# Modulation columns of the first attention in three ranges, and a new order of steps on the engines around both attentions

## What is computed

```python
c_act = jax.nn.silu(c)
for i in range(DEPTH):                       # DEPTH = 2
    mod = (c_act @ w_ada[i] + b_ada[i])[:, None, :]
    sh_a, sc_a, g_a, sh_m, sc_m, g_m = jnp.split(mod, N_MOD, axis=-1)
    h = x * (1.0 + sc_a) + sh_a
    y = diff_attention(h, ...) if i % 2 == 0 else sliding_window_attention(h, ...)
    x = layer_norm(ALPHA * x + (1.0 + g_a) * y, ln_mix_g[i], ln_mix_b[i])
    h = x * (1.0 + sc_m) + sh_m
    y = squared_relu_mlp(h, w_up[i], w_down[i])
    x = layer_norm(ALPHA * x + (1.0 + g_m) * y, ln_mlp_g[i], ln_mlp_b[i])
return x
```

## Time and profile before

| | us |
|---|---|
| median of 3 runs (2266.6 to 2270.5) | 2270.3 |
| the profiled execution | 2269.6 |
| its span, first to last instruction | 2267.5 |
| PE busy in the span | 2196.9 (97%) |
| DVE busy | 1636.5 (72%) |
| ACT busy | 987.8 (44%) |
| mean granted TensorE clock | 0.992 of full |

### The profile page before, as it was taken

The page is one execution under the profiler, slowest core; times in us unless marked ns, Lnnn a source line. Parts: engine busy times, 40 slices in busy tenths (PEclk is TensorE's granted clock), DMA queues, the critical chain, the costliest instruction groups (busy, mean ns, idle before and its releaser), DMA issues.

```text
span 2267.5 us, 26074 instructions
## 1 busy us (share of the span) xinstructions
PE 2196.9 (97%) x10140; PEld 1822.1 (80%) x10140; DVE 1636.5 (72%) x1734; ACT 987.8 (44%) x1334; POOL 33.9 (1%) x53
## 2 busy tenths in 40 slices
PE   5899999999999999999999899999999999999997
PEld 5777888887888888888887688877888888888885
DVE  5888888887887686778686888886664455564557
ACT  0134444445433443443444646536533443443542
POOL 0000000000000000000000000000000000000000
PEclk9989999999999999999999999999999999999999
DMA  9978888877998989799876765566666676666673
GB/s 373 385 284 324 319 314 295 305 238 268 332 334 287 334 318 323 268 348 328 311 256 197 243 227 201 195 194 196 223 223 219 207 241 205 213 214 220 220 230 110
DMA packets 253583, 596.42 MB, mean 263 GB/s; under 512 B 13378, under 2 KB 14740, under 8 KB 253204
## 3 DMA queue, kind: packets, MB, share of 16 engines
q1 hardware_dynamic: 244688, 578.86, 73.4%
q10 hardware_dynamic: 8772, 15.89, 2.2%
HBM read 592.60 MB, written 2.10 MB: 262 GB/s over the span
## 4 chain that ended last, share of the span: by engine, by line
PE 89%; DVE 6%; DMA 2%; issue 1%; ACT 1%; ACTq 0%; POOL 0%; DVEq 0%; POOLq 0%
PE pair L1572 24%; PE pair L1574 24%; PE pair L1573 24%; DVE acc L859 1%; PE pair L1842 1%; PE pair L1844 1%; PE pair L1843 1%; PE turn L1477 1%; DVE w_lo L837 1%; PE pair L1592 1%; PE turn L1916 1%; PE turn L1897 1%; DMA sink<-in_b_sinks_dram 1%; PE pair L1594 1%; PE pair L1593 1%
## 5 line engine op out<-in xcount | busy, mean ns | idle before, releaser
L837 DVE TENSOR_TENSOR w_lo<-raw,w_hi 128x1024 fp32r<-128x1024 f32 x712 | 851.7, 1219 | 261.6 <-ACT w_hi L470 255.0
L470 ACT ACTIVATE w_hi<-raw 128x1024 fp32r<-128x1024 f32 x712 | 729.1, 1058 | 601.3 <-PE pair L1574 420.4
L1572 PE MATMUL pair<-w_hi,h_hi 128*128 128x512 f32 x1456 | 581.1, 399 | 3.3 <-DVE w_lo L837 3.3
L1574 PE MATMUL pair<-w_hi,h_lo 128*128 128x512 f32 x1456 | 568.7, 391 | 0.0
L1573 PE MATMUL pair<-w_lo,h_hi 128*128 128x512 f32 x1456 | 567.7, 390 | 0.0
L1572 PE MATMUL pair<-w_hi,f_hi 128*128 128x512 f32 x1056 | 413.9, 392 | 0.0
L1574 PE MATMUL pair<-w_hi,f_lo 128*128 128x512 f32 x1056 | 411.2, 389 | 0.0
L1573 PE MATMUL pair<-w_lo,f_hi 128*128 128x512 f32 x1056 | 410.8, 389 | 0.0
L859 DVE SCALAR_TENSOR_TENSOR acc<-ada_w,cvec,acc 128x1024 f32<-128x1024 f32 x300 | 383.5, 1278 | 0.1
L1572 PEld LDWEIGHTS pair<-w_hi,h_hi 128*128 128x128 f32 x1456 | 274.0, 188 | 60.0 <-DVE w_lo L837 4.2
L1574 PEld LDWEIGHTS pair<-w_hi,h_lo 128*128 128x128 f32 x1456 | 273.7, 188 | 58.4
(11 more groups left out here) (184 smaller groups left out, 1651.4 us busy)
## 6 DMA issues: line engine op xcount, KB each, us to landing
ada_w<-in_w_ada_dram SPq DMA_DIRECT2D x320, 512.0 KB, 6.0
raw<-in_w_up_dram SPq DMA_DIRECT2D x128, 1024.0 KB, 5.5
raw<-in_w_down_dram SPq DMA_DIRECT2D x128, 1024.0 KB, 5.3
raw<-in_a_w_qkv_dram SPq DMA_DIRECT2D x48, 1024.0 KB, 7.2
ada_f<-in_w_ada_dram SPq DMA_DIRECT2D x44, 512.0 KB, 11.3
raw<-in_b_w_qkv_dram SPq DMA_DIRECT2D x20, 1024.0 KB, 5.2
raw<-in_a_w_o_dram SPq DMA_DIRECT2D x16, 1024.0 KB, 6.1
raw<-in_b_w_o_dram SPq DMA_DIRECT2D x16, 1024.0 KB, 5.2
```

The costliest lines, as they stand in the source:

```text
L470: act.activation(w_hi[:, (b.n * SUB + n) % SPLITS], raw[:, slot, k:k + 2], ACT.Copy).then_inc(hi_ready, 1)
L837: dve.tensor_tensor(w_lo[:, slot, k:k + 2], raw[:, slot, k:k + 2], w_hi[:, (b.n * SUB + n) % SPLITS].bitcast(F32), ALU.subtract).then_inc( ...
L1572: pe.matmul(o, hi[:, kt, at], w[:, k], start=kt == 0, stop=False)
L1574: mm = pe.matmul(o, lo[:, kt, at], w[:, k], start=False, stop=kt == KT - 1)
```

## The change

**Start.** The modulation is made in six streams instead of four: shift and scale of columns 0 to 7 in pieces of one row tile by 1024 columns as before, then shift and scale of columns 8 to 11, and of 12 to 15, in pieces of two row tiles by 512 columns, still 512 KB each. There are six `sum_end`, the last four with 4 matmuls each. The pieces that PE takes are listed by number. DVE adds a piece of the later streams with two 512-wide instructions that are linked by a semaphore. Subtiles 8 to 11 need columns 8 to 11, and 12 to 15 need 12 to 15. h of chunks 2 and 3 is handed over in halves. ACT splits 6 subtiles, not 4, before the first `first_hi`. x is loaded in two halves. The loads of the layer-norm vectors and biases move from ACT's queue to SP's, behind the first 12 pieces, and those of mask and rope tables to SP's behind piece 47; the exponential of the condition runs on ACT before the lambda and sink loads are issued. PE takes pieces 1, 4, 7, 10 before it turns the vectors.

**Elsewhere.** DVE's `block_` runs its hooks ahead of the `ada_tile`. Around the second attention two affine steps move behind `rope_k`, `rope_q` runs behind the unit steps of its subtile, and PE's and ACT's steps for the turned q move by one subtile.

```diff
+PRE_STREAMS = [(0, 0, 8), (1, 0, 8), (0, 8, 4), (1, 8, 4), (0, 12, 4), (1, 12, 4)]
+PE_PIECES = [1, 4, 7, 10, 17, 20, 23, 26, 34, 37, 41, 44, 50, 53, 57, 60]
+def pre_subtile(s):
+    if s < 8:
+        return s // 4, s % 4
+    return (s - 8) // 2 % 2, 4 + 2 * ((s - 8) // 4) + s % 2
+FIRST_SPLITS = 6
+FIRST_ADA = [6, 7]
...
             # SP
-            load_pre(16)
-            sp.dma_start(x[:], ...)
-            load_pre(14)
-            load_half(0, 0)
-            load_pre(4)
-            load_half(0, 1)
-            load_pre(6)
-            load_half(0, 2)
-            load_pre(6)
-            load_half(0, 3)
-            load_pre(14)
-            load_half(1, 0)
-            load_pre(4)
...
+            load_pre(PRE_SLOTS)
+            sp.wait_ge(cleared, 2)
...
+            load_pre(12)
+            load_x(0)
+            load_pre(8)
+            load_half(0, 0)
+            load_half(0, 1)
+            load_x(1)
+            load_half(0, 2)
+            load_half(0, 3)
+            load_pre(9)
+            load_half(1, 0)
+            load_pre(3)
+            load_half(1, 1)
+            load_pre(4)
...
+            load_pre(11)
+            load_half(1, 2)
+            load_pre(5)
+            load_half(1, 3)
...
             # ACT
-            block_(n1=HALF)
+            block_(n1=FIRST_SPLITS)
             first_hi(0)
             first_hi(1)
-            block_(n0=HALF)
-            block_(n1=2)
+            block_(n0=FIRST_SPLITS)
+            block_(n1=4)
             first_hi(2)
-            block_(n0=2, n1=3)
+            block_(n0=4, n1=6)
             first_hi(3)
...
             # DVE, pre_tile
+                for k, kt in enumerate(kts):
+                    src = pre_view(n)[:, k]
+                    if kt == 0:
+                        ins = dve.tensor_scalar(dst, src, cvec[:, 0:1], None, ALU.mult)
+                    else:
+                        if k == 0:
+                            dve.wait_ge(ada_added, ADA_SLOTS + BY_PE + n - pe_pieces(n))
+                        ins = dve.scalar_tensor_tensor(dst, src, cvec[:, kt:kt + 1], dst, ALU.mult, ALU.add)
+                    if k < len(kts) - 1:
+                        link(ins)
+                ins.then_inc(ada_added, 1)
...
             # DVE, block_
+                    if hooks and n in hooks:
+                        hooks[n]()
                     for m in ada:
                         if m == n:
                             ada_tile()
-                    if hooks and n in hooks:
-                        hooks[n]()
...
             # DVE, the start
+            tiles(16)
...
+            lambda_dots()
+            tiles(5)
+            pre_out(0)
+            lambdas()
+            tiles(11)
+            pre_out(1)
+            first_scale(0, 8)
             first_u(0)
             first_u(1)
             first_lo(0)
             block_(n1=2)
             first_lo(1)
+            block_(n0=2, n1=FIRST_SPLITS)
+            tiles(6)
+            block_(n0=FIRST_SPLITS, n1=7)
+            tiles(3)
+            pre_out(2)
+            block_(n0=7)
             tiles(4)
+            constants()
+            block_(n1=4)
             tiles(3)
+            pre_out(3)
+            first_scale(8, 4)
+            first_u(2)
+            first_lo(2, 0, 2)
+            first_lo(2, 1, 2)
+            tiles(10)
+            pre_out(4)
             tiles(4)
+            block_(n0=4, n1=6)
+            tiles(2)
+            pre_out(5)
+            first_scale(12, 4)
             first_u(3)
+            first_lo(3, 0, 2)
+            first_lo(3, 1, 2)
+            block_(n0=6, ada=FIRST_ADA, hooks={7: lambda: rope_qk(0, 0, SUB + 6)})
...
             # PE, from the second sum_end on
             sum_end(1)
             sum_begin(2)
+            for s in range(3):
+                half_subtile(s)
+            sum_piece(34)
+            half_subtile(3)
             sum_piece(37)
             pe.wait_ge(x_taken, 2)
             half_subtile(4)
+            pe.wait_ge(x_loaded, 32)
+            first_turn(2)
+            half_subtile(5)
             sum_end(2)
             sum_begin(3)
+            sum_piece(41)
+            half_subtile(6)
+            sum_piece(44)
+            half_subtile(7)
+            sum_end(3)
+            sum_begin(4)
+            half_subtile(8)
+            half_subtile(9)
+            pe.wait_ge(x_taken, 4)
+            first_turn(3)
+            sum_piece(50)
             sum_piece(53)
+            sum_end(4)
+            sum_begin(5)
             sum_piece(57)
+            sum_piece(60)
+            half_subtile(10)
+            half_subtile(11)
+            sum_end(5)
+            for s in range(12, 16):
                 half_subtile(s)
...
             # second attention: ACT, DVE, PE
-            block_(hooks={0: load_affine(2), 1: load_affine(3), 4: load_qkv_bias(0), 5: v_place, 6: k_turned(0), 7: k_turned(1)})
+            block_(hooks={0: load_affine(2), 1: load_affine(3), 5: v_place, 6: k_turned(0), 7: k_turned(1)})
...
-            block_(before=rope_k, at=3, ada=ADA_B[1], hooks={2: affine(2, 2), 5: affine(2, 3)})
+            block_(before=rope_k, at=3, ada=ADA_B[1], hooks={4: affine(2, 2), 6: affine(2, 3)})
...
-                block_(before=first, at=3, ada=ADA_B[2 + i], hooks={4: second}, beside=attend_b)
+                block_(ada=ADA_B[2 + i], hooks={3: lambda: first(49 + i, (49 + i) % 2), 4: second}, beside=attend_b)
...
-                       hooks={1: turn_pair(R_b, 0, q_there(i)), 2: turn_pair(R_b, 1, q_there(i))})
+                       hooks={2: turn_pair(R_b, 0, q_there(i)), 3: turn_pair(R_b, 1, q_there(i))})
```

## The result

The changed kernel is slower than before and slower than forecast: 2275.2 us (median of 10 runs) against 2270.3, a ratio of 1.0024 with a 95% interval of 1.0016 to 1.0033, so 0.2%. The executions of the kernel before fall into two groups (of 83 on record 22 took 2266.4 to 2267.7 us and 56 took 2269.4 or more), so that single executions of one kernel can lie almost 4 us apart. The forecast was 2267.3; the time lies just past the upper end of the range, where rival B stood.

What follows compares the result with a forecast made beforehand. The kernel was taken as PE's work plus its waits and lower-clock time. Start +2.4, first attention -2.1, second -2.6 give -2.3 on 2267.5, a span of 2265.2, with 2.1 around it 2267.3 us; range 2256 to 2275.

Steps and rivals of the forecast that it cites:

- rival B: Start: PE stands still ahead of subtiles 8 and 12, more runs at the lower clock; block 2 at 159, 2275 us; chance 0.16.
- +5.0 for the clock: Subtile 8 to block 2: 5.0 us added for lower clock in one-column matmuls and a turn, bounds 0 and 8.
- Third weight tile at 61.7, PE at 67.2: Until the first subtile: tile arrives at 61.7, splits and h follow, PE starts at 67.2, 6.3 us earlier.
- the credit of 0.6 for the stretch at 249 GB/s: Loads before the first subtile: earlier DVE start recovers 0.6 of 2.0 us lost at slack queues, bounds 0 and 2.0.
- Until the sum of stream 3: Start: `sum_end(2)` at 90.4, DVE's list of 13.9 us behind it, PE standing still from 100.4 to 105.5.
- Subtile 8 at 109.5: Start: after stream 3's sum, 0.9, and 3.1 us for bias, scale, half chunks of h and `first_lo`, subtile 8 begins at 109.5.
- The stage's upper end of +8: Until block 2: stage sum +2.4 us, range -4 to +8, including 4 for low clock at the fourth group and sums.
- Pieces in two parts: DVE in the start: a piece of two linked 512-wide instructions takes 1.5 us, between 1.39 and 1.7.
- First attention -2.1, second -2.6: Attentions: moved hooks remove PE's waits of 1.2 and 0.9; affine work behind `rope_k` removes 2.5, net -2.6 there.
- Base of the sum: Whole kernel: terms were added to the profiled span of 2267.5 us; the runs' median, 0.7 above, was left in the range.
- A: Start: stream 3 is ready after subtile 7 and the clock holds; block 2 at 139 to 141, 2256 us; chance 0.22.
- C: Attentions: nothing gained beyond the 2.1, since work moved behind `rope_k` returns at the first q; 2269.9 us; chance 0.14.

Runs made afterwards that it cites:

- e_split4: The changed kernel with ACT splitting four subtiles, not six, ahead of the first `first_hi`: 2273.0 us, ratio 1.0004 to 1.0023 against the kernel before.
- e_dve: The changed kernel with three `w_lo` and the constants on DVE moved from ahead of the fourth modulation sum to behind h of chunk 2: 2272.5 us.
- e_sum2: The changed kernel with PE's third modulation sum one subtile and one turn earlier, right after subtile 4: 2272.7 us.
- e_inter: The changed kernel with PE's pieces 50, 53, 57 and 60 each between subtiles instead of in two pairs: 2269.1 us.
- e_hooks: The kernel before with only DVE's hooks moved ahead of the `ada_tile`, second attention unchanged: 2267.1 us.
- e_attn: The kernel before with only the edits outside the start: hooks ahead of the `ada_tile` and the moved steps of the second attention: 2264.6 us.
- c_all: The changed kernel with the edits of e_split4, e_sum2, e_dve and e_inter together: 2264.4 us, ratio 0.9965 to 0.9983 against the kernel before.

## Why the prediction was wrong

The steps that failed are the price of the lower clock until block 2, put at 5.0 us beside the low subtiles, to which the runs added 6.0 (1.0, 2.1 and 2.9 below), and the third weight tile, 2.1 us late.

- **Third weight tile at 61.7, PE at 67.2.** Failed, by 2.1 and 2.0. The chain behind the tile was right (5.5 us forecast, though its terms add up to 5.3, and 5.4 measured). What failed is the credit of 0.6 for the stretch at 249 GB/s, taken because DVE starts earlier. DVE did start 5.9 us earlier, but then stood 7.1 us for pieces, since the queues moved less. By the stretches, relative to 405 GB/s, before lost 2.3 us from 10 to 25 and after 3.8; with the credit that is the 2.1. I had bounded this at 0 from below. The start was nevertheless not where the time went: e_split4 gave PE 4.1 us and kept 1.8.
- **Until the sum of stream 3.** Right in mechanism and size. `sum_end(2)` began at 91.56 (90.4), DVE waited 5.08 (6), its list lasted 14.2 (13.9), PE stood still for 4.85 (5.1). e_dve and e_sum2 show that the order on DVE makes this wait.
- **Subtile 8 at 109.5.** 111.74: 1.3 are left of the late start at `sum_end(3)`, and 1.0 comes since the sum behind the wait ran at the lower clock (1.86 for 8 matmuls, where the one at 91.56 took 0.95), which I had left to the upper bound.
- **+5.0 for the clock.** The term that was mis-sized, in two places. Until `sum_end(5)` 27.7 were forecast and 29.8 measured: the 13.6 us at the lower level there, with PE busy throughout, cost 6.8 where I had 5.0, and subtile 8 took 0.3 more. And I gave subtile 8 its 4.7 behind a wait, but took the last four at 10.9, though subtile 12 stands behind the same wait of 3.08: they took 13.9. Of the 7.4 us at block 2, 2.0 are the tile and the rest, but for 0.3, low clock: 1.0, 2.1 and 2.9, partly set against 0.9 that the first subtiles took less. The stage's upper end of +8 had 4 for low clock at the fourth group and the sums, but not the 3 up to my own bound of the clock beside them; +9.8 was measured, outside. e_inter gives back 4.9 us of clock and 1.7 of waits by the order of the same pieces.
- **Pieces in two parts.** 1.58 from start to start, forecast 1.5, bounds 1.39 and 1.7. Right. The two halves cost 0.19 us more than a wide one. The prediction's 0.14 for this compared a row that reads `pair`, which is in PSUM, with one that reads SBUF; in after, the same operation from SBUF takes 0.751 at 512 columns and 1.285 at 1024, so two halves are 0.22 us longer. That is of the kind that the Trainium skill, VectorE: DVE Perf Modes, section "The TRN2 errata", describes as a fixed time for each instruction; what the semaphore between the halves adds is not told apart from it.
- **First attention -2.1, second -2.6.** -1.9 and -2.4 by the begin of block 48 in e_hooks and e_attn. Right in mechanism and size.
- **Base of the sum.** The span of the profiled execution had its own luck of 2 us in the same stage (149.4 against 147.3 and 147.1). I had looked only at 0.7 between profile and median.
- **Rivals.** B came nearest, block 2 at 159 and 2275 against 159.22 and 2275.2, but its agreement to 0.2 us is luck. Of the subtiles that it had at the lower clock beside mine, 9 and 11 ran at the full one (2.77 and 2.72 us). Subtile 12 ran low as it said (5.26, and 0.3 more in 13). The rest was the sum behind the wait, which B had only as "sums too", the longer price of pieces 50 to 60, and the late tile, which B did not have. I gave it 0.16, because I read the fall of the clock as a price already paid before. A fell: `sum_end(3)` waited, as DVE's list said it would. C fell with e_attn. The mistake was to put the further low-clock costs into the upper end, as if each could come alone, though they came together. Whether they have one cause is not shown: one stretch began in a row of pieces with PE busy, one when a wait of 4.85 us ended, one in a wait of 3.08.

## What to carry over

When an edit gathers one-column matmuls, turns and short waits on TensorE, price that stretch and the first subtile behind a wait of 3 us at the lower clock, all of it in the forecast and not in the bound. In every profile here the subtile behind such a wait took 4.2 to 5.3 us instead of 2.72. Try the order with wide matmuls between, and look for waits ahead of it: it kept the clock in e_inter and not behind the 4.00 us of c_all. In this kernel the finer pieces moved the bound to the engine that adds them, so write out such an engine's list between two hand-overs first, and expect part of the time won ahead of a hand-over to be lost as a longer wait. Compare stages between profiles of the same program before a difference of 1 or 2 us in one of them is read as a cause.

## What was not expected of the hardware

- A TensorE that is busy 17.00 of 17.00 us, partly with one-column float32 matmuls, had a granted clock of 0.60; with the same pieces between subtiles these 17 us had 1.00 while PE was busy for 15.01. Behind a wait of 4.00 us the same order had 0.50 for 10.2 us.
- Two executions with the same instructions up to block 2 met the fall of the clock at other points, which moved block 2 by 2.1 us (149.43 and 147.34).
- Six loads of 16 to 48 KB ahead of the weights' further loads, in the same queue or in the other, made no difference (2275.2 and 2274.7), while in both kernels the queues moved little for 5 us, 232 and 238 GB/s.
